# Interleaving the high and low parts of stationary operands and issuing 512-column products whole, in a one-layer decoder on TensorE

## The reference

```
h = RMSNorm(x)
y = h @ w_in            # 3608 columns for the mixers, 6144 for three gates
y_a = sliding-window attention, y_b = stick-breaking attention, y_c = sparse attention
merged = sigmoid(g_a) * (y_a @ w_br_a) + sigmoid(g_b) * (y_b @ w_br_b) + sigmoid(g_c) * (y_c @ w_br_c)
x = x + merged @ w_out
h = RMSNorm(x)
x = x + (silu(h @ w_gate) * (h @ w_up)) @ w_down      # hidden width 5632
out = RMSNorm(x)
```

## Time and profile before

| | |
|---|---|
| median of 3 runs | 1384.86 us (1381.95 to 1387.43) |
| span of the profiled execution | 1378.3 us (the profile gives no other time of that execution) |
| TensorE busy, share of the span | 1364.8 us, 99%, 11280 matmuls |
| weight loads busy | 1332.1 us, 97% |
| VectorE busy | 922.5 us, 67% |
| ScalarE busy | 702.5 us, 51% |
| DMA | 261.08 MB, mean 189 GB/s |
| granted TensorE clock | 0.999 mean |

### The profile page before, as it was taken

How to read it: one execution, slowest core, us unless ns; L and a number is a source line. 1 busy time by engine, 2 the same in 40 slices (tenths; PEclk the granted TensorE clock), 3 DMA queues, 4 the chain that set the end, 5 groups by cost and what they waited for, 6 DMA issues and landing times.

```text
span 1378.3 us, 26427 instructions
## 1 busy us (share of the span) xinstructions
PE 1364.8 (99%) x11280; PEld 1332.1 (97%) x11280; DVE 922.5 (67%) x1189; ACT 702.5 (51%) x912; POOL 46.2 (3%) x70
## 2 busy tenths in 40 slices
PE   8999999999999999999999999999999999999997
PEld 8999999999999999999999999999999999999997
DVE  6455557667654657666788788875446788887554
ACT  7333356656545654465654555454334455545444
POOL 4000010000000110000000000000000000000111
PEclk9999999999999999999999999999999999999999
DMA  7777755455565767546556756566556665666653
GB/s 255 245 217 217 212 148 154 140 151 141 152 192 163 198 204 221 179 163 200 165 181 198 219 171 196 185 208 210 195 195 181 191 211 172 196 194 231 210 195 123
DMA packets 135264, 261.08 MB, mean 189 GB/s; under 512 B 8448, under 2 KB 25408, under 8 KB 134768
## 3 DMA queue, kind: packets, MB, share of 16 engines
q1 hardware_dynamic: 133328, 251.89, 59.8%
q0 software_dynamic: 1792, 7.57, 1.5%
q10 hardware_dynamic: 32, 0.01, 0.0%
HBM read 257.33 MB, written 2.10 MB: 188 GB/s over the span
## 4 chain that ended last, share of the span: by engine, by line
PE 89%; DVE 8%; ACT 1%; issue 1%; ACTq 0%; POOL 0%; DVEq 0%; POOLq 0%
PE bank L638 24%; PE bank L639 23%; PE bank L640 23%; PE bank L877 5%; PE bank L880 4%; PE bank L879 4%; PE bank L627 2%; DVE weight_lo_ring L1269 2%; DVE weight_sums_lo L1289 1%; DVE weight_sums L1278 1%; PE bank L776 1%; DVE act_rows L1329 1%; ACT weight_hi_ring L1039 1%; PE bank L687 1%; DVE raw_ring L1280 1%
## 5 line engine op out<-in xcount | busy, mean ns | idle before, releaser
L1269 DVE TENSOR_TENSOR weight_lo_ring<-raw_ring,weight_hi_ring 128x1024 fp32r<-128x1024 f32 (+2 forms) x480 | 581.0, 1220 | 317.0 <-ACT weight_hi_ring L1039 263.4
L1039 ACT ACTIVATE weight_hi_ring<-raw_ring 128x1024 fp32r<-128x1024 f32 (+2 forms) x432 | 449.1, 1052 | 348.6 <-PE bank L640 281.1
L638 PE MATMUL bank<-weight_hi_ring,hT_hi 128*128 128x256 f32 (+2 forms) x1280 | 384.5, 300 | 0.8 <-DVE weight_lo_ring L1269 0.8
L639 PE MATMUL bank<-weight_lo_ring,hT_hi 128*128 128x256 f32 (+2 forms) x1280 | 378.0, 295 | 0.0
L640 PE MATMUL bank<-weight_hi_ring,hT_lo 128*128 128x256 f32 (+2 forms) x1280 | 377.8, 295 | 0.0
L638 PEld LDWEIGHTS bank<-weight_hi_ring,hT_hi 128*128 128x128 f32 x1280 | 241.1, 188 | 12.5 <-issue 7.5
L639 PEld LDWEIGHTS bank<-weight_lo_ring,hT_hi 128*128 128x128 f32 x1280 | 240.5, 188 | 4.5
L640 PEld LDWEIGHTS bank<-weight_hi_ring,hT_lo 128*128 128x128 f32 x1280 | 240.4, 188 | 4.7
L638 PE MATMUL bank<-weight_hi_ring,h2T_hi 128*128 128x256 f32 x704 | 196.3, 279 | 2.2 <-DVE weight_lo_ring L1269 2.1
L640 PE MATMUL bank<-weight_hi_ring,h2T_lo 128*128 128x256 f32 x704 | 195.3, 277 | 0.0
L639 PE MATMUL bank<-weight_lo_ring,h2T_hi 128*128 128x256 f32 x704 | 195.2, 277 | 0.0
(11 more groups left out here) (238 smaller groups left out, 1883.2 us busy)
## 6 DMA issues: line engine op xcount, KB each, us to landing
raw_ring<-in_w_in SPq DMA_DIRECT2D x96, 512.0 KB, 3.6
raw_ring<-in_w_gate SPq DMA_DIRECT2D x88, 512.0 KB, 4.3
raw_ring<-in_w_up SPq DMA_DIRECT2D x88, 512.0 KB, 4.2
raw_ring<-in_w_down SPq DMA_DIRECT2D x88, 512.0 KB, 4.1
raw_ring<-in_w_in SPq DMA_DIRECT2D x56, 452.0 KB, 3.7
raw_ring<-in_w_out SPq DMA_DIRECT2D x32, 512.0 KB, 3.9
raw_ring<-in_w_br_c SPq DMA_DIRECT2D x16, 256.0 KB, 3.9
raw_ring<-in_w_br_a SPq DMA_DIRECT2D x16, 256.0 KB, 6.7
```

What stands on the lines that cost most here:

```text
L638: pe.matmul(dst, x_hi, w_hi, start=opening, stop=False, skip_group_check=True)
L639: pe.matmul(dst, x_hi, w_lo, start=False, stop=False, skip_group_check=True)
L1039: act.activation(whi[:, s, :, 0:width(u)], raw[:, s, :, 0:width(u)], ACT.Copy).then_inc(hi_ready, 1)
L1269: dve.tensor_tensor(lo, w, hi.bitcast(F32), ALU.subtract).then_inc(lo_ready, 1)
```

## The change

High and low parts of a stationary operand become one tensor whose innermost dimension has two elements, high and low; the old names are views with a step of two elements (8 bytes). This holds for hT, yT, h2T, actT and the sums of h2, for those who write them and for the loads. Every row of tokens starts at byte 192 of a line for the high part, as before, and at byte 196 for the low one (192 before). The moving operands are not touched and are read from their first column to their last as before. In `products` the two parts of 256 columns go: one product covers the width of the unit, 512 or 452 columns. `into` is not changed and keeps 256.

```diff
+def hi_and_lo(t):
+
+    if len(t.shape) == 4:
+        return t[:, :, :, 0], t[:, :, :, 1]
+    return t[:, :, :, :, 0], t[:, :, :, :, 1]
...
-        hT_hi = place("hT_hi", [KD, S], F32R)
-        hT_lo = place("hT_lo", [KD, S], F32R)
+        hT_hi, hT_lo = hi_and_lo(place("hT", [KD, S, 2], F32R)[:, :, :, :])
...
-        yT_hi = place("yT_hi", [2, 4, S], F32R)
-        yT_lo = place("yT_lo", [2, 4, S], F32R)
+        yT_hi, yT_lo = hi_and_lo(place("yT", [2, 4, S, 2], F32R)[:, :, :, :, :])
...
-        h2T_hi = at("h2T_hi", [KD, S], mid, F32R)
-        h2T_lo = at("h2T_lo", [KD, S], mid + 4 * KD * S, F32R)
+        h2T_hi, h2T_lo = hi_and_lo(at("h2T", [KD, S, 2], mid, F32R)[:, :, :, :])
...
-        actT_hi = follow_on("actT_hi", [KH, S], F32R)
-        actT_lo = follow_on("actT_lo", [KH, S], F32R)
+        actT_hi, actT_lo = hi_and_lo(follow_on("actT", [KH, S, 2], F32R)[:, :, :, :])
...
-        h2S_hi = follow_on("h2_sums_hi", [len(SEVEN), 4, P], F32R)
-        h2S_lo = follow_on("h2_sums_lo", [len(SEVEN), 4, P], F32R)
+        h2S_hi, h2S_lo = hi_and_lo(follow_on("h2_sums_split", [len(SEVEN), 4, P, 2], F32R)[:, :, :, :, :])
...
-                parts = [(0, Q4), (Q4, W)] if width == W else [(0, width)]
-                for k, t, (a, b) in [(k, t, part) for k in range(UK) for t in tiles for part in parts]:
+                a, b = 0, width
+                for k, t in [(k, t) for k in range(UK) for t in tiles]:
                     dst = bank[2 * pair + t][:, a:b]
...
-                    opening = first and k == 0 and a == 0
+                    opening = first and k == 0
                     pe.matmul(dst, x_hi, w_hi, start=opening, stop=False, skip_group_check=True)
                     pe.matmul(dst, x_hi, w_lo, start=False, stop=False, skip_group_check=True)
                     m = pe.matmul(dst, x_lo, w_hi, start=False, stop=last and k == UK - 1, skip_group_check=True)
```

## The result

The changed kernel takes 1399.68 us (median of 4 runs, 1399.37 to 1400.06), the kernel before 1383.40 us beside it (4 runs, 1380.97 to 1387.43). The ratio is 1.0106, 95% interval 1.0082 to 1.0131: the change costs 16 us. I had forecast a gain of 34. (Of all the executions in this document a single one, of e13, took 3531 us; the ratios leave it out.) The profiled execution took 1399.95 us with a span of 1398.2, 19.9 above the span of the earlier trace rows.

The account below looks back on a forecast made before the run. The prediction took the nanoseconds between starts of TensorE matmuls as the bound. Terms -30.7 - 9.3 + 0 + 3 + 3 = -33.9 us on a span of 1378.3 gave 1344.4; with 6.6 added, 1351 us, range 1320 to 1412.

Parts of the forecast that it names:

- Step (1): Lines 638 to 640: 7872 half products become 3936 whole; 227.8 ns a pair against floor 215, top 234.1.
- Step (2): Stationary reads stepping 8 bytes match the moving read's pace, leaving a quarter of the surcharge: whole product 220 ns, -30.7 us.
- the two rhythms: Same 256-column product starts every 113.6 or 117.8 ns by place; taken to show the two reads' relative position matters.
- Step (3): The 768 products of 452 and 444 columns, not regrouped, each lose 12.1 ns of surcharge: -9.3 us.
- Step (4): The 1947 up-stage products stay at 256 columns, under their load's 113 ns: 0 us, from -2 to +7.
- the load itself slows: Rival: load at 1.5 times, 160 ns, outlasts 256-column products: +99 us, 1450 us; chance 0.12.
- Step (5): VectorE and ScalarE write and re-read split operands with a step of 8 bytes: +3 us, 0 to +6.
- Step (6): Feeders get less time; gate units give a third of their gain to weight_lo_ring waits: +3 us, 0 to +8.
- The surcharge stays: Rival: reads still meet for the same time; whole product 231.7 to 234.1 ns, 1406 to 1423 us; chance 0.18.

Follow-up runs that it names:

- e13: e1 with stationary rows starting at byte 320 instead of 192, moving rows still at 128: 1387.26 us, ratio 1.0027.
- e5: Kernel before, each 512-column unit cut at a width that changes from unit to unit, operands apart: 1508.6 us, ratio 1.0926.
- e8: e5 with loads of 32 token columns instead of 128, except for the product that opens a bank: 1399.26 us, ratio 1.0102.
- e18: e1 with every moving operand of `products` reading its first column over and over: 1334.01 us, ratio 0.9643.
- e1: Kernel before with 512-column products whole, high and low parts kept apart: 1399.22 us, ratio 1.0102.
- e15: e1 with all four operands of `products` read as bfloat16, upper two bytes at a step of four: 1369.08 us, ratio 0.9899.
- e16: e1 with stationary rows at byte 128, like the moving rows (distance 0): 1387.93 us, ratio 1.0024.
- e3: Changed kernel with moving columns, and the bank's, taken from last to first: 1404.28 us, ratio 1.014.
- e14: Changed kernel with moving rows at byte 0 instead of 128: 1409.92 us, ratio 1.0194.
- e10: e5 with the stationary parts interleaved as in the change: 1540.24 us, ratio 1.1119.
- e2: Kernel before with operands interleaved, products kept in halves of 256 columns: 1433.44 us, ratio 1.0349.

## Why the prediction was wrong

- **What bounds the kernel** was right: intervals of TensorE and nothing else. That a half "can't start sooner" than its load was not what held it: the load alone would let it start after 108 to 112 ns (e5), and with a quarter of the load it stays at 114 (e8). A half walks as slowly as a whole product, 113.3 for 106.7 ns of columns, and only happens to be as long as its load. A pair of halves, 226.7, therefore had no load to be freed from, and a whole product, which walks too, had no way to the 220 that I gave it.
- **Step (1)** had both ends right: floor 215 (e18: 216.3), top 234.1 (e1: 233.5), "and a loss" for operands kept apart.
- **Step (2) is the one that failed**: "The load therefore gets in the way of the stream", and a step of 8 bytes at "equal pace" takes three quarters of that away. Of the 18.5 ns over the floor in e1, about 12 are the moving read's own: they are there in bfloat16 (e15), with a quarter of the load (e8), at the best distance (e16: 226.7 in the down projection), and go, to within 1.3 ns, only when the moving read doesn't walk (e18). The rest, 6 to 7 ns, does hang on where the two reads stand, as I took from the two rhythms; but pace and direction (e3) don't bring it, and interleaving recovers half of it only at one distance (e14). The argument leaned on line 802, a plain f32 product without loss; at half the rate its walk costs nothing either, so it could not tell the load from the walk. The term, -30.7, came out +9.2 (230.6 against 228.3 a pair, which I had put at 227.8).
- **Step (3)**: -9.3, measured 0 (370 and 370 ns); same cause.
- **Step (4)** failed as well: "0" (-2 to +7), measured +11.4, more than the failed term (2) cost. The load did slow, by 7 ns of record and 8 to 10 under narrow products (e10), and halves behind such loads start 120 ns apart throughout (e2), so the rival *the load itself slows* was right in kind at an eighth of its 51 ns. The Trainium skill's "SBUF — State Buffer" (the passage on cachelines) holds two accesses to a 16-byte line enough for full bandwidth; the load with exactly two shows 195 ns against 188, so here that isn't quite so. That halves at distance 0 are at 119.7 with contiguous loads of 191 (e16) says that position alone can cost them as much.
- **Step (5)**: +3, measured 0.9 on L1095, which the page's chain does not name. **Step (6)**: +3, measured nothing, since TensorE got no faster. Where it did, in e18, 8.5 us of waits for weight_lo_ring stand before the h2T units, the upper end of my 0 to +8.
- **The rivals.** *The surcharge stays* had the place and the sign; its whole product, 231.7 to 234.1, came at 230.6, and its 6 us of (5) and (6) did not come, while the up stage took 11.4 where it allowed up to 7; so the time was 1399.7 and not 1406 to 1423. That 1399.7 lies inside 1320 to 1412 all the same is owed to the width of that range and not to the forecast, which was 1351. It is also what the rows said most plainly: the pace of the 452-column products was measured, and only an inference stood against carrying it over to 512.

What stays open is why a walking read loses one part in sixteen (213.3 to 226.7 at 512 columns, 106.7 to 113.3 at 256), whether it would without any load beside it, and by which rule the distance acts; e8 shows only that a shorter load takes 1 to 2 ns away.

## What to carry to other kernels

Dividing a 512-column float32r product in halves costs nothing as long as the half is as long as its load: two loads hidden, 228.3 a pair against 227.7 to 233.3. A cost that looks like a wait for a partner can be the product's own pace; two numbers that agree, 113 for the load and 113 for the half, do not say which one binds. Carry a measured interval per column over to the new width before you believe a mechanism that removes it, and test the mechanism with the suspected partner taken away (e8, e18), which is one run each. Where both operands of a product start in memory is worth 12 us in 1400 here, by the distance between them (64 and 320 bytes did the same), and has its own best value for each width.

## What the runs showed of the hardware

- A moving operand that walks through its row with a step of 4 bytes, in float32r or as bfloat16, takes 226.7 to 233.3 ns for 512 columns at a granted clock of 1.00; one that reads the same column again takes 216.3. A half of 256 columns takes 113 to 114 with a load of 128 or of 32 columns beside it, at the best distance.
- The distance between the starts of the two operands moves 512 columns from 227.7 (0) to 233.2 ns (64) and 256 columns from 114.8 (64) to 119.7 (0); 192 is second best for both. At distance 64 the untouched up stage still ranges from 114.3 to 116.8 ns.
- Reading and writing backwards costs 256-column products with operands apart 4 ns (113.4 to 117.7 in the down projection), though the load beside them is the same; with interleaved operands it takes 2 ns off those of the up stage (120.1 to 117.8).
- A 128-column load with a step of 8 bytes has a record of 195 ns against 188, and under narrow products costs 8 to 10 ns more.
- VectorE's writes with a step of 8 bytes took 683 ns for 512 columns, as before; ScalarE's 625 against 586.
